# All up-projection blocks of a hybrid decoder layer in token form, with word planes written by ScalarE and transposed by the load queue

## What is computed

```
h = rms_norm(x, ffn_norm)                                  # 256 x 1024
u = causal_depthwise_conv(h @ w_up, conv_w, conv_b)        # 256 x 5632, width 3 along the tokens
u_gate, u_val = split(u, 2, axis=-1)                       # 2 x 2816
x = x + (silu(u_gate) * u_val) @ w_down                    # 2816 -> 1024
```

## Time and profile before

| | us |
|---|---|
| median of three timed runs | 455.39 |
| the profiled execution: time | 455.79 |
| the profiled execution: span, first to last instruction | 454.0 |
| TensorE busy | 449.9 (99%) |
| VectorE busy | 323.6 (71%) |
| ScalarE busy | 257.0 (57%) |
| GpSimd busy | 59.1 (13%) |
| DMA queue of SP, share of 16 engines | 60.0% |

### The profile page before, as it was taken

The page is one execution under the profiler, slowest core; times in us unless marked ns, Lnnn a source line. Parts: engine busy times, 40 slices in busy tenths (PEclk is TensorE's granted clock), DMA queues, the critical chain, the costliest instruction groups (busy, mean ns, idle before and its releaser), DMA issues.

```text
span 454.0 us, 7430 instructions
## 1 busy us (share of the span) xinstructions
PE 449.9 (99%) x2957; PEld 411.7 (91%) x2957; DVE 323.6 (71%) x397; ACT 257.0 (57%) x362; POOL 59.1 (13%) x49
## 2 busy tenths in 40 slices
PE   8999999999999999999999999999999999999997
PEld 6889888888888999999999888999999999888886
DVE  4789994876689848772469566678888888889423
ACT  6885453055996668324435356467676767566300
POOL 0100021599450021210000003000000000000000
PEclk9999999999999999999999999999999999999999
DMA  8997658558999426995546345745444455446002
GB/s 286 423 410 248 237 188 228 140 185 224 252 270 297 164 93 203 270 307 241 186 186 250 121 185 186 234 185 187 185 185 185 185 185 185 186 180 246 38 0 94
DMA packets 40268, 93.50 MB, mean 206 GB/s; under 512 B 26929, under 2 KB 27825, under 8 KB 30897
## 3 DMA queue, kind: packets, MB, share of 16 engines
q1 hardware_dynamic: 39824, 91.55, 60.0%
q0 software_dynamic: 416, 1.57, 1.0%
HBM read 85.77 MB, written 1.05 MB: 191 GB/s over the span
## 4 chain that ended last, share of the span: by engine, by line
PE 92%; DMA 4%; DVE 2%; SPq 1%; issue 1%; ACT 1%
PE bank L557 16%; PE bank L559 16%; PE bank L558 16%; PE bank L511 6%; PE bank L509 6%; PE bank L510 6%; PE bank L781 4%; PE bank L782 4%; PE bank L784 4%; DMA w_raw<-weights_dram 4%; PE bank L696 2%; PE bank L694 2%; PE bank L695 2%; PE bank L639 1%; PE bank L652 1%; DVE area L1108 1%
## 5 line engine op out<-in xcount | busy, mean ns | idle before, releaser
L1081 DVE TENSOR_TENSOR w_pair<-w_raw,w_pair 128x2048 fp32r<-128x2048 f32 x73 | 168.8, 2324 | 45.7 <-ACT w_pair L801 45.2
L801 ACT ACTIVATE w_pair<-w_raw 128x2048 fp32r<-128x2048 f32 x73 | 138.4, 1921 | 29.9 <-PE bank L559 15.2
L557 PE MATMUL bank<-h_hi,w_pair 128*128 128x256 f32 x448 | 125.5, 280 | 0.0
L558 PE MATMUL bank<-h_lo,w_pair 128*128 128x256 f32 x448 | 125.1, 279 | 0.0
L559 PE MATMUL bank<-h_hi,w_pair 128*128 128x256 f32 x448 | 125.1, 279 | 0.0
L558 PEld LDWEIGHTS bank<-h_lo,w_pair 128*128 128x128 f32 x448 | 84.2, 188 | 0.1
L557 PEld LDWEIGHTS bank<-h_hi,w_pair 128*128 128x128 f32 x448 | 84.2, 188 | 0.1
L559 PEld LDWEIGHTS bank<-h_hi,w_pair 128*128 128x128 f32 x448 | 84.2, 188 | 0.0
L557 PE MATMUL bank<-a_hi,w_pair 128*128 128x256 f32 x192 | 53.9, 281 | 0.2 <-DVE w_pair L1081 0.2
L558 PE MATMUL bank<-a_lo,w_pair 128*128 128x256 f32 x192 | 53.6, 279 | 0.0
L559 PE MATMUL bank<-a_hi,w_pair 128*128 128x256 f32 x192 | 53.6, 279 | 0.0
(11 more groups left out here) (157 smaller groups left out, 626.0 us busy)
## 6 DMA issues: line engine op xcount, KB each, us to landing
w_raw<-weights_dram SPq DMA_DIRECT2D x73, 1024.0 KB, 5.4
w_raw<-weights_dram SPq DMA_DIRECT2D x8, 256.0 KB, 5.4
w_raw<-weights_dram SPq DMA_DIRECT2D x4, 512.0 KB, 9.1
ys<-x_dram SPq DMA_DIRECT2D x2, 512.0 KB, 9.2
xs<-x_dram POOLq DMA_DIRECT2D x1, 1024.0 KB, 7.8
area<-decay_dram SPq DMA_DIRECT2D x1, 768.0 KB, 8.3
out_dram<-ys SPq DMA_DIRECT2D x3, 256.0 KB, 2.0
xs<-x_chan_dram SPq DMA_DIRECT2D x1, 512.0 KB, 6.9
```

What stands on the lines that cost most here:

```text
L557: mm(o, s_hi, r_hi[:, k, :], start=(k == 0 and m % 2 == 0), stop=False)
L558: mm(o, s_hi, r_lo[:, k, :], start=False, stop=False)
L801: A(w_parts(n, r)[0], raw[r][:, :], ACT.Copy).then_inc(hi_ready, 1)
L1081: tt(lo, raw[r][:, :], hi.bitcast(f32), ALU.subtract).then_inc(lo_ready, 1)
```

## The change

All eleven up blocks are done in token form. For each block ScalarE reads each of the two banks once and writes the two 16-bit words of its values straight into two planes (`up_tok_read`); GpSimd has no part any more. SP's queue, between the weight loads, transposes both planes of a block (`turn_up`, one DMA per token tile). One block later VectorE joins the words into `u_in` (`up_join`, two instructions) and ScalarE does the last tap from SBUF (`up_scale`, four instructions, then as before taps, SiLU, product and split). The product overwrites the value part of `conv`. The loops of ScalarE, VectorE and SP are written out; TensorE's is one loop of five turns. Weights of up and down blocks all lie shifted, and the down weights are no longer rotated. The up blocks run tile by tile: tile 0 with both halves, then tile 1 with both; the first half of a block is free after three quarters of it.

```diff
-                moving = n // 2 in TOKEN_BLOCKS or n >= DOWN_FIRST_HALF + 2
+            moving = not isinstance(n, int) or n // 2 in TOKEN_BLOCKS or n >= 2 * UP0
...
+            def turn_up(b, t):                                              # SP
+                wait_bank_read(sp, UP0 + b, t)
+                if b >= 2:
+                    sp.wait_ge(up_in_ready, 2 * (b - 2) + t + 1)
+                sp.dma_start(up_turned[b % 2][t].rearrange("p (b s) -> p b s", s=P), up_planes[b % 2][t], transpose=True)\
+                    .then_inc(up_was_turned[b % 2][t], 16)
+            for n in range(UP_LOADS, HALVES):
                 sp.wait_ge(lo_ready, n - SLOTS + 1)
                 sp.dma_start(raw[n % SLOTS][:, :], weights[n]).then_inc(raw_loaded[n % SLOTS], 16)
+                b, t = divmod(n - (UP_LOADS + 3), NT)
+                if 0 <= b < UP_BLOCKS:
+                    turn_up(b, t)
...
+            def up_tile(n, slot, jj, free, t, h):                           # TensorE
+                if t == 0:
+                    pe.wait_ge(lo_ready, n + 1)
+                if h == 0:
+                    pe.wait_ge(bank_read[jj], free)
...
+                for kk in range(4):
+                    k = 4 * h + kk
+                    s_hi, s_lo = (part[:, k, P * t:P * t + P] for part in (h_hi, h_lo))
+                    mm(o, s_hi, hi[:, kk, :], start=(k == 0), stop=False)
+                    mm(o, s_hi, lo[:, kk, :], start=False, stop=False)
+                    ins = mm(o, s_lo, hi[:, kk, :], start=False, stop=(k == KT - 1))
+                if t == 1:
+                    ins.then_inc(half_used, 1)
+                elif h == 1:
+                    ins.then_inc(up_summed, 1)
...
+            def up_tok_read(b, t):                                          # ScalarE
+                if t == 0:
+                    act.wait_ge(up_summed, b + 1)
+                else:
+                    act.wait_ge(half_used, 2 * (UP0 + b) + 2)
+                if b >= 2:
+                    act.wait_ge(up_was_turned[b % 2][t], 16 * (b // 2))
+                A(up_planes[b % 2][t].rearrange("p (w c) -> p w c", w=2),
+                  block_bank(UP0 + b, t)[:, :].bitcast(u16).rearrange("p (c w) -> p w c", w=2), ACT.Copy)
+            def up_scale(b):
+                act.wait_ge(up_in_ready, 2 * b + 2)
+                if b >= 2:
+                    act.wait_ge(a_split, b - 1)
...
+                        ins = A(conv[:, b % 2, m, :], u_in[:, b % 2, m, PAD:PAD + SEQ], ACT.Identity,
                                 scale=col[:, c + 2:c + 3], bias=col[:, c + 3:c + 4])
+            for b in range(UP_BLOCKS + 1):
+                n = 2 * (UP0 + b) + 4
                 split(n)
+                if b < UP_BLOCKS:
+                    up_tok_read(b, 1)
+                split(n + 1)
+                if b >= 2:
+                    up_high(b - 2)
+                if b >= 1:
+                    up_scale(b - 1)
+                if b + 1 < UP_BLOCKS:
+                    up_tok_read(b + 1, 0)
+                if b >= 1:
+                    up_silu(b - 1)
+            up_high(UP_BLOCKS - 1)
+            for n in range(DOWN_FIRST_HALF + 6, HALVES):
+                split(n)
...
+            for b in range(UP_BLOCKS + 1):                                  # VectorE
+                n = 2 * (UP0 + b) + 4
                 split(n)
+                split(n + 1)
+                if b >= 1:
+                    up_join(b - 1)
+                if b >= 2:
+                    up_low(b - 2)
+                if b >= 1:
+                    up_conv(b - 1)
+            split(DOWN_FIRST_HALF + 6)
+            up_low(UP_BLOCKS - 1)
+            for n in range(DOWN_FIRST_HALF + 7, HALVES):
+                split(n)
```

More of the change, by code:

```diff
@@ L34 @@
  OUT0, OUT1, UP0) = range(23)
-TOKEN_BLOCKS = (V_R0, V_R1, G_R0, G_R1, Q_M0, Q_M1, K_M0, K_M1, V_M0, V_M1, OUT0, OUT1, UP0)
+TOKEN_BLOCKS = (V_R0, V_R1, G_R0, G_R1, Q_M0, Q_M1, K_M0, K_M1, V_M0, V_M1, OUT0, OUT1)
 DOWN_FIRST_HALF = 2 * (UP0 + UP_BLOCKS)
@@ L133, in hybrid_layer @@
         discard = a_hi[:, 2 * KT:2 * KT + 4, :].rearrange("p k (i c) -> p (k i) c", c=P)
-        prod = area[:, 6144:7168].rearrange("p (b m s) -> p b m s", b=2, m=2)
+        prod = conv[:, :, 2:4, :]
         x_tok = xs[:, :].rearrange("p (t d) -> p t d", t=NT)
@@ L146, in hybrid_layer @@
         ret_turned = [area[:, 2048 + 1024 * t:3072 + 1024 * t].bitcast(u16) for t in range(NT)]
-        up_planes = [y_tok[:, t, 512:1024].bitcast(u16) for t in range(NT)]
-        up_turned = [area[:, 7168 + 512 * t:7680 + 512 * t].bitcast(u16) for t in range(NT)]
+        up_planes = [[part.bitcast(u16) for part in parts]
+                     for parts in ([y_tok[:, t, 512:1024] for t in range(NT)],
+                                   [area[:, 6160 + 512 * t:6672 + 512 * t] for t in range(NT)])]
+        up_turned = [[area[:, 4112 + 1024 * jj + 512 * t:4624 + 1024 * jj + 512 * t].bitcast(u16) for t in range(NT)]
+                     for jj in range(2)]
         PAIR = 2 * 3 * P
@@ L221, in hybrid_layer @@
         pads_ready = sem("pads_ready")
-        up_planes_ready = sem("up_planes_ready")
-        up_was_turned = [sem(f"up_was_turned{t}") for t in range(NT)]
+        up_was_turned = [[sem(f"up_was_turned{jj}{t}") for t in range(NT)] for jj in range(2)]
         up_in_ready = sem("up_in_ready")
@@ L337, in _ @@
             LAST_TURN = 2 * GATE_R1 + 9
-            ROUNDS = (HALVES - SLOTS) // SLOTS
             def turn_gates(q):
@@ L479, in _ @@
                     .then_inc(inv_x2_ready, 1)
[L481 to L485, removed]
         @block.tensor
@@ L735, in _ @@
                         ins.then_inc(half_used, 1)
-            def up_half(b, n, free, slot, jj, h):
-                pe.wait_ge(lo_ready, n + 1)
+            def up_tile(n, slot, jj, free, t, h):
+                if t == 0:
+                    pe.wait_ge(lo_ready, n + 1)
                 if h == 0:
                     pe.wait_ge(bank_read[jj], free)
[L742 to L751, removed]
+                hi, lo = (w.rearrange("p (k c) -> p k c", k=4) for w in w_parts(n, slot))
+                o = bank[2 * jj + t][:, :]
+                for kk in range(4):
[8 more added lines that the diff above has]
+                    ins.then_inc(up_summed, 1)
+            with pe.Fori(0, UP_BLOCKS // 2) as i:
+                for jj in (1, 0):
+                    first = 2 * UP0 + (2 if jj else 4)
+                    read_first = UP0 - 2 if jj else UP0
+                    for t in range(NT):
+                        for h in range(2):
+                            up_tile(i * 4 + (first + h), (first + h) % SLOTS, jj, i * 2 + (read_first + t + 1), t, h)
             for j in range(DOWN_HALVES):
@@ L995, in _ @@
             h2_high(1)
-            up_tok_read(0)
+            up_tok_read(0, 0)
             split(2 * UP0 + 3)
[L998 to L1026, removed]
+            def up_scale(b):
+                act.wait_ge(up_in_ready, 2 * b + 2)
+                if b >= 2:
+                    act.wait_ge(a_split, b - 1)
@@ L1035, in _ @@
-            nc.scalar.preload_act_table(ACT.Silu)
[L1036 to L1055, removed]
-                split(n)
[L1057 to L1060, removed]
+            def up_silu(b):
+                act.wait_ge(conv_gate_done, b + 1)
+                A(conv[:, b % 2, 0:2, :], conv[:, b % 2, 0:2, :], ACT.Silu).then_inc(silu_done, 1)
@@ new lines, in up_high @@
+            def up_high(b):
+                act.wait_ge(prod_ready, b + 1)
+                A(a_hi[:, 2 * b:2 * b + 2, :], prod[:, b % 2, :, :], ACT.Copy).then_inc(a_hi_ready, 1)
+            nc.scalar.preload_act_table(ACT.Silu)
+            for b in range(UP_BLOCKS + 1):
+                n = 2 * (UP0 + b) + 4
+                split(n)
+                if b < UP_BLOCKS:
[9 more added lines that the diff above has]
+                    up_silu(b - 1)
@@ L1420, in _, with up_join, up_conv @@
             dve.wait_ge(pads_ready, 2)
-            def up_conv(jj, read, silu, conv_col, conv_steps):
+            steps0 = done[0]
+            def up_join(b):
+                for t in range(NT):
+                    dve.wait_ge(up_was_turned[b % 2][t], 16 * (b // 2 + 1))
+                    nc.vector.tensor_copy(
+                        u_in[:, b % 2, :, PAD + P * t:PAD + P * t + P].bitcast(u16).rearrange("p m (s w) -> p w m s", w=2),
+                        up_turned[b % 2][t].rearrange("p (w m s) -> p w m s", w=2, m=4)).then_inc(up_in_ready, 1)
+            def up_conv(b):
+                jj = b % 2
                 for j in range(2):
-                    dve.wait_ge(*read(j))
+                    dve.wait_ge(up_scaled, 2 * b + j + 1)
                     for tap in (1, 0):
@@ L1428, in up_conv @@
                             m = 2 * j + i
+                            c = COL_CONV + 16 * b + 4 * m + tap
                             ins = stt(out=conv[:, jj, m, :], in0=u_in[:, jj, m, tap:tap + SEQ],
```

(44 more changed lines are left out.)

29 lines of the change are left out of this document (8 added, 21 removed).

## The result

| | runs | median us | range | against the kernel before, with its 95% interval |
|---|---|---|---|---|
| before | 22 | 455.62 | 455.01 to 457.82 | |
| changed | 22 | 457.67 | 456.31 to 460.14 | 1.004 [1.0028, 1.0051] |

What follows compares the result with a forecast made beforehand. TensorE was taken to bound the kernel before; after the change, rounds of 11.97 us against its 10.90 make its 5.01 us of waiting eat its 3.3 us gain. Span 455.72 us, median 457.1 us, range 453.0 to 462.6.

Steps and rivals of the forecast that it cites:

- The bound changes hands: Up blocks: TensorE sets the end before; after, ScalarE and VectorE need 11.97 us a round against its 10.90.
- TensorE's part: Matmuls of twenty-two halves: each goes from 5.60 to 5.45 us, 3.3 us gained if nothing else ends later.
- The ring: Up blocks: ScalarE's and VectorE's in-order lists wait for each other in a circle, 11.97 us a round.
- the read: ScalarE reading 1024 16-bit words, every second one, out of a bank: taken as 1.00 us, bounds 0.94 and 1.25.
- my own case: Up blocks: the circle of waits with a read of 0.94 to 1.10 us, 456 to 459 us; chance 55%.
- the path over the taps: End of a round: through VectorE's taps instead of ScalarE's last taps and read, 11.94 us a round.
- The sum: Rounds followed to down half 6, which starts at 425.72 us; span 455.72 us, 1.72 more than before.
- TensorE's four waits: TensorE waits before down halves 0, 2, 4 and 6 of about 0.4, 1.1, 1.0 and 2.5 us.
- The clock: Rival, 10%: TensorE's waits lower its clock, or transposes hold up weights; one half at 1.2 GHz costs 5.45 us: 462.6.
- What was costed at nothing: Transfers hidden, 9.0 us in a round of 11.97; GpSimd off the path; written-out loops change no instruction's work.
- The rival on the other side: Up blocks: busy sums decide and TensorE stays the bound, span 450.7 us, time 452.1 us; chance 11%.
- the lead: Start of the up blocks: round 1's second half is ready 8 us before TensorE wants it.

Runs made afterwards that it cites:

- e1_join_first: The changed kernel with VectorE joining block b-1 before the two splits of its round instead of behind them: 452.64 us, 0.9931 against the kernel before.
- e4_before_shift: The kernel before with the 8-element shift in every weight slot, channel-form blocks too: 461.38 us, 1.0126 against the kernel before.

## Why the prediction was right, step by step

**The bound changes hands.** Right: TensorE set the end before; in the rounds of the change ScalarE and VectorE wait for each other, and TensorE for them.

**TensorE's part.** 5.44 us a half in the up blocks, as taken from the token-form row. `e1_join_first`, where nothing else is in the way, shows the gain in time: 3.2 us between the medians, 3.3 forecast. Its span is 3.6 us shorter than that of the profiled execution before (450.4 against 454.0); the rest goes outside the span. By the formula of the Trainium skill, "TensorE: Matmul & The Clock Gate", section "Back-to-back issue gap", which is said there to be that of a matmul by itself, the gain would be an estimated 1.3 to 1.4; the trace does not agree, with 0.227 and 0.117 us a matmul for its 0.216 and 0.109.

**The ring.** Right in its links, and 0.18 us too long: 11.79 us a round for 11.97. The mis-sized term is the read: 0.90 us start to start where I took 1.00, just below the 0.94 to 1.10 of my own case. Of the bounds the lower one was nearest (0.94 from two copies of floats): every second word out of a bank goes at about the pace of floats, and the 16-bit row with its strided output is no guide to them. By the Trainium skill, "ScalarE: Activation LUTs", section "What ACT_TABLE_LOAD costs", it is an estimated 0.95 to the next start; the trace has 0.90, so it agrees within 0.05 us. Join to last taps is 0.04 us, not 0.10, and the path over the taps, 11.94 us in the prediction, is the longer one at the end of the ring.

**The sum.** Eight rounds of 0.18 us put half 6 some 1.4 us too late: it starts 426.16 - 280.84 = 145.32 us after UP0, where 425.72 - 279.01 = 146.71 was forecast. Of TensorE's four waits, the last is near the size foreseen (2.8 for 2.5), the earlier ones together 1.0 where 2.5 were. By the ring alone the median would then be 455.7 us. The group with the full clock has 456.57; of the 0.9 us between them 0.2 are the kernel before itself, at 455.62 in 22 runs and 455.39 in the three of the forecast, and half lies outside the span.

**The clock.** I had a fall of the clock as a rival, at 10% and 5.45 us. It happens, in about half of the executions, beside the ring rather than in place of it, and costs some 1.6 us in the profiled one; the two groups' medians lie 1.3 us apart (456.57 and 457.87).

**Outside the span.** The forecast kept this time as it was. It grew by some 0.47 us, and not by the ring: `e1_join_first` has it too (2.20 to 2.30 us), `e4_before_shift`, with the loops of the kernel before, has not (1.74 to 1.81). What it goes to is not shown; the loops written out are common to all kernels that have it.

**What was luck.** The ring's sum was 1.4 us too large; the 0.47 us outside the span stood nowhere, and the clock, 1.1 us in the median (457.67 against 456.57), only among the rivals. They nearly cancel, so the forecast's 457.1 against 457.67 flatters its sum. So does the direction: on the prediction's scale a round of 11.76 us brings no change and one of 11.87 a loss clear of noise, so the ring at 11.79 would by itself have been too near to no change to tell. Mechanism and place were right by the working.

**What was costed at nothing.** Right inside the span: transposes land 5.9 us after issue in the median and nobody waits for them; VectorE's and ScalarE's lists written out show no idle time beside waits for each other and for TensorE; GpSimd is not missed.

**The rival on the other side.** That busy sums decide was wrong for the change, by the order in the lists alone. With the joins first the sums are the same and they do decide: 452.64 us, where that rival's time was 452.1.

## What to carry to other kernels

Before a stage is moved to two engines with in-order lists, follow the waits once round from each list to the other and back and add up start-to-start times: busy sums under the bound say nothing if that circle is longer. A circle only a little longer than the bound costs its excess per round once the lead is spent, so the number of rounds decides, and moving instructions ahead of those that wait can be worth as much as shortening one of them: the joins first gave 452.64 us, half of the read 452.65. Look at what stands last in each list too: the end of a pipeline can add a wait of its own. And a wait of TensorE can cost a second time where its clock falls behind it, here 1.6 us after one of 2.5.

## What the runs showed of the hardware

- After a wait of 2.5 us TensorE ran at 1.2 GHz for some 3 us in both profiled executions of the changed kernel; the mean clock of 0.996 that goes with it stands in 18 of its 34 executions. With eight matmuls of unused work in that wait it stands in none of eleven. A wait of 0.6 us before half 4 was followed by no such stretch in the four traces that have it.
- Shifting the weights by 8 elements makes the same matmul faster or slower by some 3% with the operand's part: 0.117 to 0.120 us for 256 columns with the weights stationary, (402.21 - 391.00) / 48 = 0.234 to 0.227 us for 512 with the weights moving.
- ScalarE reads 1024 16-bit words two apart out of a bank in 1.00 us and writes them packed; 2048 words read packed from SBUF and written two apart take 2.53 us (two in 4.93). Whether the stride of the output or the source makes the difference was not tried.
